# A three-layer transformer block on one core: the MLP's matmuls are read and written in 64-byte pieces, and seven buffers get a chosen start line

## The reference, cut to what matters

```
x = first_block(...)      # a retention layer, then latent attention (MLA), each with layer norm
                          # x = LN(alpha * x + layer(x))
# second_block:
x = x + concat(pool_mixer(u), neighbourhood_attention(q, k, v)) @ w_out
h = rmsnorm(x, norm_mlp_g)
x = x + square(relu(h @ w_up)) @ w_down        # w_up 1024 x 4096, w_down 4096 x 1024
return rmsnorm(x, final_g)
```

## Time and profile before

| | us |
|---|---|
| median of 3 runs | 1546.25 |
| the profiled execution, first to last instruction (span) | 1544.4 |
| PE busy in it | 1512.3 (98%) |
| PE weight loads busy | 1244.7 (81%) |
| DVE / ACT / POOL busy | 705.5 / 564.1 / 600.4 |

### The profile page before, as it was taken

How to read it: one execution, slowest core, us unless ns; L and a number is a source line. 1 busy time by engine, 2 the same in 40 slices (tenths; PEclk the granted TensorE clock), 3 DMA queues, 4 the chain that set the end, 5 groups by cost and what they waited for, 6 DMA issues and landing times.

```text
span 1544.4 us, 19587 instructions
## 1 busy us (share of the span) xinstructions
PE 1512.3 (98%) x7260; PEld 1244.7 (81%) x7260; DVE 705.5 (46%) x1060; ACT 564.1 (37%) x961; POOL 600.4 (39%) x259
## 2 busy tenths in 40 slices
PE   7999999999999999999999999899999999999998
PEld 6888888888778888888888878688778888888886
DVE  5454544434624554455545543725856111143435
ACT  4323232322355434343334332534754323232222
POOL 4434343445433323222322244434544444354542
PEclk9999999999999999999999999999999999999999
DMA  7222222232322122212221443243012232323231
GB/s 281 82 89 81 88 81 88 81 109 81 106 92 77 63 99 72 72 54 98 71 71 60 171 173 109 82 138 121 28 52 99 82 108 82 109 82 109 81 109 55
DMA packets 27062, 146.25 MB, mean 95 GB/s; under 512 B 2960, under 2 KB 3344, under 8 KB 12176
## 3 DMA queue, kind: packets, MB, share of 16 engines
q1 hardware_dynamic: 23136, 133.25, 24.7%
q10 hardware_dynamic: 3888, 12.49, 2.3%
HBM read 138.39 MB, written 7.34 MB: 94 GB/s over the span
## 4 chain that ended last, share of the span: by engine, by line
PE 86%; issue 5%; DVE 4%; POOL 3%; ACT 1%; DMA 0%; SPq 0%; POOLq 0%; ACTq 0%; DVEq 0%
PE bank L378 26%; PE bank L379 26%; PE bank L380 26%; POOL wlo L460 3%; PE bank L758 1%; PE bank L752 1%; PE bank L768 1%; DVE h_tok L1393 1%; PE bank L754 1%; PE bank L757 1%; PE bank L755 1%; DVE xlo L1334 1%; PE bank L891 0%; DVE win L1670 0%; DVE h_tok L1377 0%
## 5 line engine op out<-in xcount | busy, mean ns | idle before, releaser
L460 POOL TENSOR_TENSOR wlo<-stage,whi 128x1024 fp32r<-128x1024 f32 (+1 forms) x224 | 564.1, 2541 | 887.6 <-ACT whi L943 879.6
L943 ACT ACTIVATE whi<-stage 128x1024 fp32r<-128x1024 f32 (+1 forms) x222 | 224.5, 1060 | 355.1 <-PE bank L380 350.8
L378 PE MATMUL bank<-xhi,whi 128*128 128x512 f32 (+1 forms) x760 | 295.1, 388 | 10.0 <-DVE xlo L1334 9.9
L380 PE MATMUL bank<-xhi,wlo 128*128 128x512 f32 (+1 forms) x760 | 291.5, 384 | 0.0
L379 PE MATMUL bank<-xlo,whi 128*128 128x512 f32 (+1 forms) x760 | 291.3, 383 | 0.0
L378 PEld LDWEIGHTS bank<-xhi,whi 128*128 128x128 f32 x760 | 143.2, 188 | 42.4 <-POOL wlo L460 10.3
L380 PEld LDWEIGHTS bank<-xhi,wlo 128*128 128x128 f32 x760 | 143.2, 188 | 28.5
L379 PEld LDWEIGHTS bank<-xlo,whi 128*128 128x128 f32 x760 | 143.4, 189 | 26.7
L1334 DVE TENSOR_TENSOR dr_lo<-hid,dr_hi 128x512 fp32r<-128x512 f32 x32 | 64.9, 2068 | 101.8 <-ACT dr_hi L946 101.8
L378 PE MATMUL bank<-whi,xhi 128*128 128x512 f32 (+1 forms) x256 | 97.8, 382 | 4.4 <-POOL wlo L460 3.4
L379 PE MATMUL bank<-wlo,dr_hi 128*128 128x512 f32 x256 | 100.9, 394 | 0.0
(11 more groups left out here) (263 smaller groups left out, 2803.8 us busy)
## 6 DMA issues: line engine op xcount, KB each, us to landing
stage<-in_w SPq DMA_DIRECT2D x104, 1024.0 KB, 4.8
stage<-in_w SPq DMA_DIRECT2D x8, 1152.0 KB, 5.9
o_spill<-gt SPq DMA_DIRECT2D x16, 256.0 KB, 6.1
bT<-o_spill SPq DMA_DIRECT2D x4, 1024.0 KB, 8.1
xres<-in_xT SPq DMA_DIRECT2D x8, 256.0 KB, 6.2
xres<-in_x ACTq DMA_DIRECT2D x1, 2048.0 KB, 8.9
rows<-in_ln ACTq DMA_DIRECT2D x2, 1024.0 KB, 5.2
h_tok<-v_spill ACTq DMA_DIRECT2D x8, 256.0 KB
```

The lines of the kernel that those rows point to most:

```text
L378: pe.matmul(dst, a_hi, b_hi, start=start, stop=False)
L380: return pe.matmul(dst, a_lo, b_hi, start=False, stop=stop)
L460: pool.tensor_tensor(wlo[p % 2][:, r], stage[p % 2][:, r], whi[p % 2][:, r].bitcast(F32), ALU.subtract).then_inc(w_lo, 1)
L943: act.activation(whi[p % 2][:, r], stage[p % 2][:, r], ACT.Copy).then_inc(w_hi, 1)
```

## The change

`by_line` rewrites 512 columns as 8 groups (b) of 4 pieces (a) of 16 columns. Column a * 128 + b * 16 + r is visited in the order b, a, r: first columns 0 to 15, 128 to 143, 256 to 271, 384 to 399, then 16 to 31, and so on. In SBUF each piece is one 64-byte line, and the four pieces of a group have the same class. The PSUM tile is walked in the same order, so that each column lands where it did. It is used in the 672 matmuls of the up loop and in the 720 of `half` in the down projection; the 16th panel of the down projection goes straight through as before.

Gaps are empty buffers of whole lines. One line each ahead of ar, c, br and cr moves them, and what follows them in their context (ql, kr, wkr, qn, kn, vb, pt and others), from class 1 to class 2. Seven lines ahead of relu move relu and dr from class 1 to class 0. gap_x and gap_ql are of size 0.

```diff
+        def gap(name, lines, where=ctx):
+            if lines:
+                sb(name, [P, 16 * lines], F32, where)
...
+        gap("gap_x", 0)
         xhi = sb("xhi", [P, KX, SEQ], F32R)
...
+            gap("gap_ar", 1, h)
             ar_hi = sb("ar_hi", [P, 4, SEQ], F32R, h)
...
+            gap("gap_c", 1, h)
             c_hi = sb("c_hi", [P, KC, SEQ], F32R, h)
...
+            gap("gap_ql", 0, h)
...
+            gap("gap_br", 1, h)
...
+                gap("gap_cr", 1, f)
...
             hid = sb("hid", [P, KF, SEQ], F32, h)
+            gap("gap_dr", 7, h)
             relu = sb("relu", [P, 4, SEQ], F32, h)
...
+        def by_line(x):
+
+            return x.rearrange("p (a b r) -> p b a r", a=4, b=8, r=16)
...
-                        last = split_dots(pe, parts[m][:, :], wh[:, k, c], wl[:, k, c],
-                                          moving[0][:, k, :], moving[1][:, k, :], k == 0, k == nk - 1)
+                        last = split_dots(pe, order(parts[m][:, :]), wh[:, k, c], wl[:, k, c],
+                                          order(moving[0][:, k, :]), order(moving[1][:, k, :]), k == 0, k == nk - 1)
...
-                                last = split_dots(pe, bank[2 * q + c][:, :], hi[:, kk % 4, r], lo[:, kk % 4, r],
-                                                  wh[:, b, w], wl[:, b, w], first and kk == 0, False)
+                                last = split_dots(pe, order(bank[2 * q + c][:, :]), hi[:, kk % 4, r], lo[:, kk % 4, r],
+                                                  order(wh[:, b, w]), order(wl[:, b, w]), first and kk == 0, False)
...
-                          lambda m: pe.wait_ge(u_r, 4 * i + (2 * a + m + 1)), u_m)
+                          lambda m: pe.wait_ge(u_r, 4 * i + (2 * a + m + 1)), u_m, order=by_line)
             project_out(DN, KF, dr_hi, dr_lo, HA * VT + HB + KX,
-                        lambda q: pe.wait_ge(u_r, KF + min(4, 2 * q + 2)))
+                        lambda q: pe.wait_ge(u_r, KF + min(4, 2 * q + 2)), order=by_line)
```

More of the change, by code:

```diff
@@ L522, in need, with tiles @@
                     pe.wait_ge(w_lo, 2 * n + (2 * p + 1 + (k > 0)))
-            def tiles(p, n, nk, parts, moving, lo, hi, before, signal, each=False):
+            def tiles(p, n, nk, parts, moving, lo, hi, before, signal, each=False, order=lambda x: x):
                 wh, wl = panel(p, nk)
@@ L598, in first_product, with project_out @@
                 half(1, 3).then_inc(signal, 1)
-            def project_out(p0, nk, hi, lo, a0, free=None, turn=None):
+            def project_out(p0, nk, hi, lo, a0, free=None, turn=None, order=lambda x: x):
                 def half(n, j, first):
```

## The result

The changed kernel has a median of 1551.05 us (18 runs, 1547.26 to 1554.34), the kernel before in the same measurement 1547.78 us. The ratio is 1.0024, 95% interval 1.0015 to 1.0033: 3.7 us more (2.3 to 5.1); the two medians themselves lie 3.3 us apart. The forecast was 1525.6 us, with 1517 to 1550 as its range.

What follows compares the result with a forecast made beforehand. PE was taken as the bound, busy 98% of the span, by the distance between matmul starts. 1544.4 - 7.2 (gaps) - 13.5 (walk) = 1523.7 us; with the median 1.85 us above the span, 1525.6 us, range 1517 to 1550.

Steps and rivals of the forecast that it cites:

- the term of the walk: Up loop and down projection: walking by lines brings matmuls to 218 ns, gaining 5.7 and 7.8 us, together 13.5.
- rival B: MLP matmuls: order changes nothing, the surplus being a fixed start cost; only the gaps pay, 1539.1 us; 12%.
- The gap term: Stages with br, ar, cr, ql and c: moved to class 2, matmuls take 226.5 ns; 7.2 us gained, 4 to 8.
- Rival D: All 1392 walked matmuls: pieces cost more than the meetings, 13.3 ns each, +18.5 - 7.2, so 1557.6 us; 18%.
- The seventh gap: Last 48 matmuls of the down projection: class 0 paired with class 2 straight through, 1 to 5 ns each, below 0.3 us.

Runs made afterwards that it cites:

- b2: The kernel before, unchanged, executed once more for a second profile; span 1548.4 us.
- e2: The changed kernel with every matmul walked straight, dr still at class 0, executed once; down projection 232.4 ns a matmul.
- m1: A kernel of its own: 96 matmuls of one shape for each of 41 settings of walk, operand distance and stationary width; straight, 128 wide, 226.7 to 233.4 ns.
- e4: The changed kernel with all seven gaps at 0, walk by lines kept; ratio 1.0056 (1.0037 to 1.0076) to the kernel before.
- e1: The changed kernel walked straight, with one line in place of seven ahead of relu and dr; ratio 0.996 to the kernel before, median 1540.43 us.
- e5: As e1, but five lines ahead of relu and dr, so dr is at class 6; ratio 0.9961 to the kernel before, median 1542.20 us.
- e3: The changed kernel with one line in place of seven ahead of relu and dr, walk kept, executed once; down projection 231.0 ns a matmul.
- m2: A kernel of its own: 96 matmuls for each of 33 settings, with other walks and shorter moving operands; straight 120.0, 173.6, 226.9 ns at 256, 384, 512 columns.

## Why the prediction was wrong

**What failed is the term of the walk**, in the words "I take 218 ns, two thirds of the surplus gone". The rows of before showed 6.8 ns to be a matter of place (for ql and c moving b2 bears it out), and I took them out of the 13.2 ns that the best-placed pair still had. They were on top: 226.5 was already the pair without the extra. The tables have no walk and no distance below 226.7 at 512 columns, and at distance 0 the 13 ns are the same at 256, 384 and 512 columns and do not shrink with a load of 16 columns. The prediction had said that a fixed cost per matmul would look alike, and then did not give rival B its due.

**The sign of the walk was wrong as well.** Up it costs 231.0 - 226.5 = 4.5 ns x 672 = 3.0 us where 5.7 us of gain stood; down, 7.1 x 720 = 5.1 us, and some 0.2 us in the 16th panel (e2's 3.5 ns x 48), where 7.8 of gain stood. The swing is 13.5 + 8.3 = 21.8 us of the 25.5 us between forecast and result. The gap term adds 2.3 us (below), and 1.5 us are the median of before, which was 1546.25 us in 3 runs and 1547.78 in 18.

**Rival D had the right place and direction and a third to half of the price**, 4.5 and 7.1 ns in place of 13.3. Of the three causes that it named, writing PSUM in pieces and reading pieces as such cost nothing (m1: 226.8 with PSUM in pieces; 230.0 with 64 stationary columns by either walk). The price was there with the 128-column load beside a moving read in pieces. Its third cause, four lines of one class in a row, is not ruled out: a longer stay in a class fits the 8-piece walk, 237 to 241 ns, but two pieces cost 240 too, so what exactly happens inside is open.

**The two rules that the prediction weighed.** The Trainium skill's rule that any non-contiguous pattern slows matmuls (Advanced Engine Details and Errata, PSUM Cachelines) would have given the right sign for the wrong reason. In m1, PSUM in 64-byte pieces, with every two elements adjacent, costs 0.1 ns. The Trainium skill's rule that PE has two independent read ports and never waits (SBUF — State Buffer, Who interferes with whom) does not fit the times measured here. With the walk and the shape unchanged, moving the stationary operand by a line changes 226.7 to 233.4 ns in m1, in a stretch in which nothing but PE runs.

**The gaps gained, but less than forecast.** By stage against b2, from the starts in the two timelines: ar to the next stage 89.4 to 88.7 us, the MLA layer 409.4 to 406.4, br 89.3 to 86.9, cr 46.2 to 45.9, together 6.4 us for the forecast 7.2. Of br's 2.4 us, however, 1.6 are the clock's, which in b2 has 0.64 from 895 to 899 us, where br begins, and does not fall there in the changed kernel. e4, with br where before has it and the clock full, takes 87.8 us, so the gap brings 0.9 there and all gaps 4.9 us. The mis-sized part is br: 6.8 ns x 384 = 2.6 us stood there, from the 233.3 ns of the one profile, where the place is worth 2.2 ns x 384 = 0.8 us. The prediction had seen that ar and br with one class and 4.6 ns between them spoke against it, and its 4 to 8 us for the term held.

**The seventh gap** I missed as well: I wrote of the down projection as if only the walk changed, and costed dr's class 0 for the 16th panel alone. Straight, distance 6 in place of 7 costs 3.5 ns (e2), 2.5 us over 720 matmuls. In the changed kernel it did no more harm than in the 16th panel, since by lines both distances take 236 to 237 ns (e4).

**Sum.** -4.9 + 3.0 + 5.1 + 0.2 = +3.4 us, against +3.7 (2.3 to 5.1) measured. For e1 it is -4.9 - 768 x 2.2 = -6.6, against -6.2 (-8.4 to -3.9), and e5 has -6.0 (-8.5 to -3.6).

**What the clock does beside it.** In the profiles, the last of the first 60 matmuls with x behind br starts 25.2 us after br's last matmul in the changed kernel, e1, e2 and e3, and after 23.3 to 23.6 us in before, b2, e4 and e5. Windows of 4 us, from 15.8 us behind that matmul on, in the changed kernel and then in e5:

```profile
994.00:998.00 4.00, 2.43 (x11) 2.24 (x12) 3.90 (x5) 2.71 (x5) 0.00 (x0) 0.74 0.00 0
998.00:1002.00 4.00, 4.00 (x16) 3.22 (x15) 2.75 (x5) 1.45 (x3) 0.00 (x0) 0.84 0.00 0
```

```profile
996.00:1000.00 4.00, 2.35 (x15) 2.09 (x16) 3.85 (x6) 2.69 (x6) 0.00 (x0) 1.00 0.00 0
1000.00:1004.00 4.00, 4.00 (x19) 3.31 (x18) 2.83 (x5) 1.45 (x3) 0.00 (x0) 1.00 0.00 0
```

In the four profiles with 25.2 us the clock is low just where PE has work and sets the pace. In before, e4 and e5 it fell earlier, ahead of a wait of PE that takes up the delay, and in b2 it did not fall there. e5 has all the gaps, so they don't force it. Whether the changed kernel meets it more often than the kernel before is open, as no experiment took the clock apart.

## What to carry to other kernels

On a kernel whose matmuls follow each other without a gap, take the distance from start to start, group the matmuls by where their two operands lie, and put pairs that meet in one matmul of 512 float32r columns at equal starts modulo 256 bytes; here 5 gaps of one line gave 0.4% (e1). Measure other lengths by themselves: at 256 columns distance 7 took 117.8 ns and distance 0 took 120.0. Take the distances of a second execution before you build a term on one: br's 233.3 ns were not there again. Do not subtract a difference between two groups from the better group's own surplus over the clock: first measure one operation alone at several lengths, which shows what is fixed. A bound stage turns a change of 4 ns into microseconds either way, so a reordering there deserves a table of single settings before it deserves a kernel.

## What the runs showed of the hardware that was not expected

- A float32r matmul with a 128-column stationary operand at distance 0 takes 13.3 to 13.6 ns over its columns at 2.4 GHz, at 256, 384 and 512 columns (m2), and 16, 32, 64, 96 and 112 stationary columns are no faster at 512 moving ones (231.1, 231.7, 230.0, 230.0, 228.9 ns against 226.7).
- At 512 columns, straight, the distance of the two operands' starts modulo 4 lines sets 226.7, 233.4, 232.4 or 228.9 ns; a stationary start off by a part of a line gives 233.3, a moving start 4 columns off 231.6.
- One execution of the unchanged program can have another distance in a stage: 233.3 ns with br in the first profile of before, 228.9 in b2 and in e4.
- PSUM was written in 64-byte pieces for 0.1 ns a matmul (m1); both operands that are walked, moving and PSUM, in 16-byte pieces at 512-byte steps cost 40 to 44 ns a matmul (267 to 271).
- Single executions of the unchanged program differ by over 4 us with the time that the clock spends at its lower level in the neighbourhood attention: 1544.4 us at mean clock 0.996, 1548.4 at 0.993 (before and b2).
